# Feed-forward stages: seven-product pairs at other steps and in greater number, with the weight sums made by accumulating transfers

## The reference

```python
def swiglu(x, w_in, w_out):
    gate, up = jnp.split(x @ w_in, 2, axis=-1)
    return (jax.nn.silu(gate) * up) @ w_out
...
x = x + 0.5 * swiglu(rms_norm(x, ffn1_norm_g[i]), ffn1_w_in[i], ffn1_w_out[i])
```

## Time and profile before

| | |
|---|---|
| median of three runs | 1537.32 us (1535.16 to 1537.65) |
| the profiled execution | 1531.57 us, its span 1529.8 us |
| granted TensorE clock | 0.999 |
| TensorE busy | 99% of the span |
| VectorE, ScalarE, GpSimd busy | 72%, 56%, 23% |
| DMA | 311.43 MB, mean 204 GB/s |

### The profile page before, as it was taken

How to read it: one execution, slowest core, us unless ns; L and a number is a source line. 1 busy time by engine, 2 the same in 40 slices (tenths; PEclk the granted TensorE clock), 3 DMA queues, 4 the chain that set the end, 5 groups by cost and what they waited for, 6 DMA issues and landing times.

```text
span 1529.8 us, 19935 instructions
## 1 busy us (share of the span) xinstructions
PE 1517.7 (99%) x7906; PEld 1292.2 (84%) x7906; DVE 1094.3 (72%) x1174; ACT 858.6 (56%) x1075; POOL 358.5 (23%) x256
## 2 busy tenths in 40 slices
PE   9999999999999999999999999999999999999998
PEld 7888888888778888888888888899988899888886
DVE  6677766557778567776776678599998566666875
ACT  7545554645365454556776456476887343464554
POOL 0352200001732135320001631100571000017320
PEclk9999999999999999999999999999999999999999
DMA  7977665457776688765416986766554665578763
GB/s 253 314 243 233 188 182 188 138 170 211 239 246 192 193 275 251 228 195 173 158 56 206 285 230 203 209 191 204 181 181 147 212 192 187 173 223 273 226 194 102
DMA packets 274309, 311.43 MB, mean 204 GB/s; under 512 B 64272, under 2 KB 233512, under 8 KB 274216
## 3 DMA queue, kind: packets, MB, share of 16 engines
q1 hardware_dynamic: 273112, 308.84, 64.4%
q10 hardware_dynamic: 1104, 1.31, 0.3%
HBM read 295.92 MB, written 1.09 MB: 194 GB/s over the span
## 4 chain that ended last, share of the span: by engine, by line
PE 90%; POOL 3%; DVE 2%; issue 2%; DMA 2%; ACT 2%; ACTq 0%; DVEq 0%; POOLq 0%
PE ps L2344 22%; PE ps L2348 22%; PE ps L2345 22%; PE ps L2334 3%; PE ps L2336 3%; PE ps L2335 3%; PE ps L2546 2%; PE ps L2545 2%; PE ps L2544 2%; DMA scr<-scr 1%; PE ps L2387 1%; PE ps L2500 1%; POOL scr L750 1%; DVE w_lo L1412 1%; POOL scr L760 0%
## 5 line engine op out<-in xcount | busy, mean ns | idle before, releaser
L1412 DVE TENSOR_TENSOR w_lo<-w_raw,w_hi 128x2048 fp32r<-128x2048 f32 x250 | 598.5, 2400 | 185.1 <-ACT w_hi L803 184.7
L803 ACT ACTIVATE w_hi<-w_raw 128x2048 fp32r<-128x2048 f32 x250 | 477.0, 1912 | 250.8 <-PE ps L2348 200.5
L2344 PE MATMUL ps<-w_hi,xg_hi 128*128 128x512 f32 (+1 forms) x960 | 375.2, 391 | 1.2 <-DVE scr L1527 1.2
L2348 PE MATMUL ps<-w_hi,xg_lo 128*128 128x512 f32 (+1 forms) x960 | 372.1, 388 | 0.0
L2345 PE MATMUL ps<-w_lo,xg_hi 128*128 128x512 f32 (+1 forms) x960 | 372.0, 387 | 0.0
L750 POOL COPY scr<-scr 128x512 uint16<-128x512 uint16 x100 | 121.1, 1231 | 697.8 <-DVE scr L1527 697.7
L2344 PE MATMUL ps<-w_hi,y_hi 128*128 128x512 f32 x666 | 261.9, 393 | 1.3 <-DVE y_lo L1532 0.7
L2348 PE MATMUL ps<-w_hi,y_lo 128*128 128x512 f32 x666 | 259.1, 389 | 0.0
L2345 PE MATMUL ps<-w_lo,y_hi 128*128 128x512 f32 x666 | 258.9, 389 | 0.0
L2344 PEld LDWEIGHTS ps<-w_hi,xg_hi 128*128 128x128 f32 x960 | 180.3, 188 | 39.1 <-DVE w_lo L1412 1.6
L2348 PEld LDWEIGHTS ps<-w_hi,xg_lo 128*128 128x128 f32 x960 | 180.3, 188 | 36.8
(11 more groups left out here) (403 smaller groups left out, 1710.8 us busy)
## 6 DMA issues: line engine op xcount, KB each, us to landing
w_raw<-in_ffn_w_in_dram SPq DMA_DIRECT2D x168, 512.0 KB, 5.0
w_raw<-in_ffn_w_out_dram SPq DMA_DIRECT2D x88, 512.0 KB, 5.5
w_raw<-in_w_in_dram SPq DMA_DIRECT2D x82, 512.0 KB, 4.6
w_raw<-in_a_w_in_dram SPq DMA_DIRECT2D x28, 512.0 KB, 4.5
w_raw<-in_w_down_dram SPq DMA_DIRECT2D x22, 512.0 KB, 5.1
w_raw<-in_w_gate_dram SPq DMA_DIRECT2D x21, 512.0 KB, 4.1
w_raw<-in_w_up_dram SPq DMA_DIRECT2D x21, 512.0 KB, 5.2
y_raw<-in_ffn_w_in_dram SPq DMA_DIRECT2D x16, 512.0 KB, 5.4
```

Of the source, the lines that this page charges most:

```text
L803: act.activation(w_hi[:, u % RING, :], w_raw[:, u % RING, :], ACT.Copy).then_inc(w_rounded, 1)
L1412: dve.tensor_tensor(w_lo[:, s, :], w_raw[:, s, :], w_hi[:, s, :].bitcast(F32), ALU.subtract).then_inc(w_split, 1)
L2344: pe.matmul(dst, xh, hi, start=start, stop=False, skip_group_check=True)
L2348: return pe.matmul(dst, xl, hi, start=False, stop=stop, skip_group_check=True)
```

## The change

Pairs now stand at step 8 in the first two stages (steps 8 and 9 are done together) and at steps 4 and 8 in the last three (4 with 5, 8 with 9). The places of the units in a stage are computed from that list. The four weight sums of a pair are made by transfers that add on their way from SBUF to SBUF (`accum_op`), issued by GpSimd; signs are arranged so that all four are additions, and one drained block is negated instead. The sums of the input move from GpSimd to VectorE, three steps ahead of the stage's first pair. SyncE's loads of the T blocks stand at other places. The queues' lists around the pair are parameterised by its step.

The stages and the order of their units:

```diff
-PAIR = 7
+PAIRS_OF = ((8,), (8,), (4, 8), (4, 8), (4, 8))
...
+            order += [("G", i, 0), ("G", i, 1), ("G", i + 1, 1), ("D", i - 1), ("G", i + 2, 0), ("G", i + 2, 1), ("D", i), ("D", i + 1)]
```

On SyncE's queue:

```diff
+                def block(p, k, j):
+                    half, i = ((0, p), (0, p + 1), (1, p + 1), (1, p))[k]
+                    if p == pairs[0]:
+                        sp.wait_ge(w_used, u + 1)
+                    else:
+                        sp.wait_ge(pe_done, pe_.at(f"M{(5, 7, 6, 4)[k]} {f} {pairs[0]}"))
+                    dst = t_raw[k].rearrange("p (k c) -> p k c", k=4)[:, :, 256 * j:256 * j + 256]
+                    sp.dma_start(dst, gu_src(f, half, i)[j]).then_inc(t_landed[k], 16)
...
+                def step(i):
+                    p = pairs[0]
+                    if i == p - 3:
+                        block(p, 0, 0)
+                        block(p, 0, 1)
+                    gate_up(1, i)
+                    if i == p - 3:
+                        block(p, 1, 0)
+                        block(p, 1, 1)
+                    down(i - 1)
+                    if i == p - 2:
+                        block(p, 3, 0)
+                    if i < NI - 1:
+                        gate_up(0, i + 1)
+                    turn_back(i - 1)
+                    if i == p - 3:
+                        block(p, 2, 0)
+                        block(p, 2, 1)
+                    if i == p - 2:
+                        block(p, 3, 1)
+                    if i + 1 in pairs[1:]:
+                        block(i + 1, 3, 0)
+                        block(i + 1, 3, 1)
...
+                def pair(p):
+                    q = pairs[1] if p + 4 in pairs else None
+                    gate_up(1, p)
+                    gate_up(1, p + 1)
+                    down(p - 1)
+                    turn_back(p - 1)
+                    gate_up(0, p + 2)
+                    gate_up(1, p + 2)
+                    if q:
+                        for k in (0, 1):
+                            block(q, k, 0)
+                            block(q, k, 1)
+                    down(p)
+                    down(p + 1)
+                    turn_back(p)
...
+                    turn_back(p + 1)
+                    if q:
+                        block(q, 2, 0)
+                        block(q, 2, 1)
```

On GpSimd:

```diff
+                def add(p, k, src):
+                    n = pair_count(f, p)
+                    if k in (T1, T3, T4):
+                        pool.wait_ge(t_landed[k], 32 * n)
+                    pool.wait_ge(*{T1: (t_landed[T3], 32 * n), T3: (t_landed[T2], 32 * n), T2: (t_added[T1], 16 * n), T4: (t_added[T2], 16 * n)}[k])
+                    if k == T3:
+                        pool.wait_ge(t_added[T1], 16 * n)
+                    if k == T2:
+                        pool.wait_ge(t_added[T3], 16 * n)
+                    pool.dma_start(t_raw[k], t_raw[src], accum_op=ALU.add).then_inc(t_added[k], 16)
...
                 for i in range(1, NI - 1):
                     cut(i)
+                    if i + 3 == pairs[0]:
+                        add(i + 3, T1, T3)
+                    if i + 2 == pairs[0]:
+                        add(i + 2, T2, T1)
+                    if i + 2 in pairs[1:]:
+                        add(i + 2, T3, T2)
                     pool.wait_ge(ffn_hl, NI * nth[f] + i)
                     join(i)
-                    if i == 1:
-                        x_sums()
-                    if i == 2:
-                        s_sums()
+                    if i + 3 == pairs[0]:
+                        add(i + 3, T3, T2)
+                    if i + 2 == pairs[0]:
+                        add(i + 2, T4, T2)
+                    if i + 3 in pairs[1:]:
+                        add(i + 3, T1, T3)
+                    if i + 2 in pairs[1:]:
+                        add(i + 2, T2, T1)
+                        add(i + 2, T4, T2)
```

On ScalarE:

```diff
+                def t_high(p, k):
+                    act.wait_ge(t_added[k], 16 * pair_count(f, p))
```

On VectorE:

```diff
+                def step(i, more=False):
+                    v = u + at["G", i, 0]
                     split(v + 2)
+                    hidden_low(i - 1, (i - 1) % 2)
...
+                    if i == pairs[0] - 3:
+                        x_sums()
+                    if i + 2 == pairs[0]:
+                        s_lows((0, 1))
+                    if i + 1 in pairs:
+                        t_low(i + 1, T1)
                     split(v + 3)
                     for tt in range(2):
                         product(i, tt)
...
+                    if i == pairs[0] - 3:
+                        s_sums()
...
+                def x_sums():
+                    dve.tensor_tensor(x_sum, xg_hi[:, :, :].bitcast(F32), xg_lo[:, :, :].bitcast(F32), ALU.add).then_inc(vec_done, vec(f"X {f}"))
...
+                def t_low(p, k):
+                    dve.wait_ge(act_done, act_.at(f"T hi {f} {p} {k}"))
+                    if k in (T1, T2):
+                        dve.wait_ge(t_added[T2 if k == T1 else T4], 16 * pair_count(f, p))
...
+                def pair(p):
+                    n = u + at["G", p, 0]
+                    t_low(p, T2)
                     split(n + 2)
+                    t_low(p, T3)
+                    t_low(p, T4)
```

More of the change, by code:

```diff
@@ L346, in build, with pair_count, alone_until, alone @@
         T1, T3, T2, T4 = range(4)
+        def pair_count(f, p):
+            return sum(len(PAIRS_OF[g]) for g in range(f)) + PAIRS_OF[f].index(p) + 1
+        def alone_until(f, i):
+            def alone(f, j):
+                return j not in PAIRS_OF[f] and j - 1 not in PAIRS_OF[f]
+            return sum(alone(g, j) for g in range(f) for j in range(NI)) + sum(alone(f, j) for j in range(i + 1))
         x_sum = tiles(KB(40, 8))
@@ L534, in ffn @@
                     small_inputs()
-                for i in range(1, PAIR):
-                    gate_up(1, i)
-                    down(i - 1)
-                    if i == 1:
[L539 to L564, removed]
+                i = 1
+                while i < NI:
+                    if i in pairs:
+                        pair(i)
+                        i += 3
+                    else:
+                        step(i)
+                        i += 1
+                if NI - 3 not in pairs:
+                    down(NI - 1)
                 if f == 4:
@@ L974, in ffn @@
                         act.activation(rope[:, j], rope[:, j], ACT.Sin).then_inc(act_done, act_(f"rope {j}"))
-                for i in range(3, PAIR):
-                    step(i)
-                pair()
-                for i in range(PAIR + 3, NI):
-                    step(i, last=i == NI - 1)
+                i = 3
+                while i < NI:
+                    if i in pairs:
+                        pair(i)
+                        i += 3
+                    else:
+                        step(i)
+                        i += 1
             def mem(n, gain):
@@ L2596, in ffn @@
                         pe.wait_ge(act_done, act_.at("M kT 1"))
-                    down(i - 1, start=i == 1)
-                pair()
-                for i in range(PAIR + 3, NI):
-                    gates(i, taken(i - 1))
-                    down(i - 1, hidden=(lambda: hidden(NI - 1)) if i == NI - 1 else None)
+                    down(i - 1, start=i == 1, hidden=(lambda: hidden(NI - 1)) if i == NI - 1 else None)
+                i = 1
+                while i < NI:
+                    if i in pairs:
+                        pair(i)
+                        i += 3
+                    else:
+                        step(i)
+                        i += 1
                 down(NI - 1, norm=n + 1)
```

286 lines of the change are left out of this document (129 added, 157 removed).

## The result

The changed kernel takes 1670.99 us (median of 4, 1665.16 to 1684.38), the kernel before 1536.24 beside it: a ratio of 1.090 [1.087, 1.094]. I had forecast 1557, with a range up to 1604.

What follows compares the result with a forecast made beforehand. TensorE, busy 99% of the span, bounds the kernel, so any lateness adds in full. -10.1 + 3 x (4.5 + 0.5 + 4.9) = +19.6 us gives 1557 from the median of 1537.3; range 1536 to 1604.

Steps and rivals of the forecast that it cites:

- The step that failed: GpSimd's queue: hidden-tile cuts and joins behind the waiting sums have a down unit and two gate units of room.
- L: Time of one link in a pair's chain of 1 MB adding transfers: 8.6 us taken, ends 5.2 and 10.5.
- The six waits over 2 us that I had forecast: TensorE in stages 3 to 5: 3.7 us inside each third gate unit, 4.0 us at each second pair.
- the second pairs: Last three stages: the split behind T2's sum 4.0 us late, T4's low part 0.9; together 4.9 us each.
- The rival of saturated engines: DMA engines saturate, an adding transfer takes 9.5 us or more; at 10.5 both pairs wait: 1606 us, chance 0.22.
- First pairs: First pair of a late stage: sums of 8.6 us arrive in time and cost nothing, up to 8.75.
- The stage start: Stages 3 to 5: u+3 lands late, the third gate unit waits 3.7 us, first down unit 4.5 later in all.
- my 4.5: Delay in us of the first down unit in each of the last three stages from u+3's late load (4.1 to 5.6).
- The gain: TensorE: three more pairs save 8.2 us of matmuls, a second-stage wait of 1.9 goes; 10.1 us in all.
- The input sums' 0.5 us: Input sums moved to VectorE, step 1 of the last three stages: 0.5 us per stage (0 to 1.5).
- Bandwidth: DMA engine time per 1 MB: 3.35 us for a load, 3.35 to 6.7 for an adding transfer.
- the rival of quick sums: Adding transfers land in 7.3 us or less, only the stage starts cost: 1542 us (1539 to 1546), chance 0.28.

Runs made afterwards that it cites:

- the repeat: The changed kernel, unchanged, profiled once more: 1678.10 us.
- the last kernel: Changed kernel with the four weight sums on VectorE, T1's and T3's loads later, and T2's low part ahead of a split: 1529.25 us, ratio 0.998.
- the run with both edits: Changed kernel with GpSimd issuing a first pair's T1 sum only after the transpose landed, and T1's and T3's loads behind the stage start's: 1625.99 us.
- one pair and the wait: Changed kernel with one pair at step 8 in every stage, and the first sum issued only when the transpose beside it has landed: 1564.47 us.
- the wait: Changed kernel with GpSimd waiting for the transposed tile before it issues T1's sum of a stage's first pair: 1638.28 us, ratio 1.067.
- Later loads alone: T1's and T3's loads behind the stage start's: 1658.99 us on the changed kernel, 1625.99 with GpSimd's wait for the transpose, 1545.30 with sums on VectorE.

## Why the prediction was wrong

**The step that failed** is the sentence "Queued behind the waiting sums on GpSimd are the cuts and joins of the hidden tiles; those have a down unit and two gate units of room there." The cuts and joins had room for an L of 8.6. I gave every adding transfer the same L and asked only who stands behind it on GpSimd's queue. I did not ask what else its landing, or the instruction just ahead of it, releases: the cut releases SyncE's transpose, so T1's sum and the transpose of a hidden tile start together, and then both take 21 to 32 us. Shown by four runs: parted in either direction (after the transpose, 1638; well ahead of it, 1617) or with nothing added (1578) there is no crawl of 20 us, and with it, in the repeat, there is. Over all runs, 20 first sums were issued 0.1 us ahead of a transpose: 17 took 13.8 to 31.7 us, and the 3 in stage 1 (T loads early) 9.6 to 9.7. Another 20 were parted from it and took 8.3 to 12.8. Each edit moves the sum against SyncE's loads too, one later and one earlier; no run moved the transpose alone. It costs 33 us by the one edit and 54 by the other, which also lets the sums of the first pairs start earlier. Why adding makes a stop of 2 us into one of 20, and why stage 1 is spared, is open. In stage 1 the first sum took 15.8 us, not 9.7, once T1's and T3's loads stood later, so what else is in flight seems to take part; that was not tried by itself.

**The clock** was missing from the sum. I priced waits by their length. The 14 stretches at granted clock 0.50 cost 1.5 to 3.1 us each, 30.9 in all. (The 4.8 us that are left of the 35.7 stand in the last kernel too, which has no such stretch.) The length of the wait hardly matters: 1.7 us behind the longest (17.1 us), 1.7 behind one of 3.2. By the traces' stretches the loss is 24.3 us in the run with both edits (11 waits over 2 us), 10.5 with one pair and the wait (6) and 8.3 with sums on VectorE (9): 2.2, 1.7 and 0.9 us per wait. Very short waits often go free: of the six of 1.9 to 2.2 us in the run with sums on VectorE and later loads three had a stretch behind them, 1.7 us each, and three had none. The six waits over 2 us that I had forecast would have come to some 13 us more at 2.2 each, 1570.

**L was undersized for the second pairs.** I took 8.6; T1's, T3's and T2's sum of the second pair in the third stage landed in 13.0, 9.3 and 10.5. T1's went out 41.3 us after the first pair's start (36.2 forecast), T2's landed at 75.2 (62.0), and behind it stood low part and split, 4.6 as forecast: 79.8 after the start, where the pair would have begun at 68.0 (62.6). The mechanism and its place were right; 11.8 us in place of 4.9 is a mis-sized term, three times over. The rival of saturated engines, L at 10.5, had 12.5 for it.

**First pairs.** Nothing was forecast up to an L of 8.75. With the crawl taken away by the wait, they cost 4.2 to 5.4 us each; the first three links took 8.7 to 11.6 us, the rival's case again. Its 1606 is not shown by that: the run nearest to it, T1's sum ahead of the cut, gave 1617, but with 18 us of half clock that the rival lacked, and with 3 to 4 us at the first pairs of stages 3 to 5 where it had 7. That the two lie close is partly luck.

**The stage start was right in its wait.** Gaps of 3.4, 3.3 and 3.8 us stood inside the third gate unit (3.7 forecast), with ScalarE's rounding of u+3 waiting for a DMA at 572.98. Later loads alone gave back 12.0, 12.3 and 14.5 us in three pairs of runs, 4.0 to 4.8 per stage, where I had 4.5. These have the half clock in them and my 4.5 had not, and only the 14.5, with no adding transfer beside it, is clear of the crawl: the wait of 3.7 was sized well, the agreement of the totals is partly luck.

**The gain was right in matmuls; its 8.2 us never showed in full.** Eight groups of seven blocks are there, 36 matmuls fewer. In the last kernel the stage of one pair whose waits I had counted, the second, is 3.0 us shorter (1.9 forecast). But from the start of the third stage to its last matmul that kernel gains 0.9 us of the 8.2; the short halts take the rest. The input sums' 0.5 us fits: the first down unit of stages 3 to 5 waits 0.1, 1.2 and 0 us.

**Bandwidth** was sized a little high: 2.8 us of the engines for a copy and 5.1 to 5.3 for a sum outside the crawl, where I had 3.35 and 6.7. L is twice that and more; whether the loads that share the engines make the difference, no run shows. The Trainium skill, DMA: Bandwidth & Descriptors, section Anatomy of one DMA, SWDGE (gpsimd) path, has the fit of 2.0 us plus bytes over 436 GB/s, by which I estimated a link of 4.4 us, the rival of quick sums. A plain copy took 7.1 to 8.6 in the medians of this crowded queue, 4.8 at the quickest. The measurement decides: the fit holds no price for what shares the engines.

## What to carry to other kernels

- Before you put a transfer on another queue, ask what the same event releases elsewhere, and price the pair. One line moved, 10 us earlier, gave 54 us.
- Price a wait of a saturated TensorE by its length and 1.5 to 3 us of half clock with it, whether it lasts 3 us or 17; waits of 2 us had it in three cases of six. To shorten a long wait, and not remove it, wins idle time only.
- Where an engine has room for an operation of 2.3 us, it beats an adding transfer of 10 in a chain; order its queue then by which product wants what first. That order was worth 16 us here.

## What was not expected of the hardware

- An adding 1 MB transfer within SBUF that starts 0.1 us ahead of a transpose can slow all DMA to 47 to 85 GB/s for 20 us, at a DMA share of 0.97 to 1.60. A plain copy at the same place stops it for some 2 us only, and an adding transfer that had been under way for 2 to 11 us did not at all. The Trainium skill, DMA: Bandwidth & Descriptors, section 🎯 Rules for kernel authors, says that a transpose next to ordinary DMAs needs nothing, in a row on what transfers in flight together do to each other's data. It says nothing there on speed, and for an adding one beside it this trace shows that speed does need distance.
- While GpSimd adds 128x2048 (4.6 to 6.6 us, 5.0 in the mean), a VectorE subtraction with both inputs in SBUF waits: 4.37 us for 0.69.
- An adding transfer takes 5.1 to 5.3 us of the 16 engines per MB (6.0 with the crawl in it), a plain one 2.8.
- TensorE lost about as much to the half clock behind a wait of 3 us as behind one of 17: 1.5 to 3.1 us.
